# A 24th buffer for expert weights in place of the attention's probabilities, and a mixer ring of four chunks instead of five

## The reference, cut to what matters

```python
proj = h @ w_in                       # 1024 x 7184, then conv, recurrence, attention
merged = sigmoid(gate_lru) * (y_lru @ w_lru_out) + sigmoid(gate_fox) * (y_fox @ w_fox_out)
x = x + merged @ w_o
...
for e in range(N_EXPERTS):            # 32
    gu = t @ w_gate_up[e] + b_gate_up[e]               # 1024 x 2048 weights
    gate = jnp.minimum(gu[:, :D_FF], SWIGLU_LIMIT)
    up = jnp.clip(gu[:, D_FF:], -SWIGLU_LIMIT, SWIGLU_LIMIT)
    y = ((up + 1.0) * gate * sigmoid(SWIGLU_ALPHA * gate)) @ w_down[e] + b_down[e]   # 1024 x 1024
    out = out + combine[:, e:e + 1] * y
```

## Time and profile before

| what | us |
|---|---|
| median of three runs (lowest, highest) | 1183.79 (1182.74, 1183.94) |
| the profiled execution | 1183.51 |
| its span, first to last instruction | 1181.73 |
| TensorE busy in the span | 1150.8 (97%) |
| VectorE, ScalarE, GpSimd busy | 339.2, 271.0, 28.3 |
| transferred by DMA | 452.92 MB, mean 383 GB/s |

### The profile page before, as it was taken

One profiled execution on the slowest core, in us unless ns is written; L12 is line 12 of the kernel. 1 busy time (PEld: TensorE's weight loads), 2 busy tenths in 40 slices (PEclk: granted clock), 3 DMA queues, 4 the chain that ended last, 5 costly groups with the idle time before them and its releaser, 6 DMA issues.

```text
span 1181.7 us, 14466 instructions
## 1 busy us (share of the span) xinstructions
PE 1150.8 (97%) x6297; PEld 590.1 (50%) x6297; DVE 339.2 (29%) x663; ACT 271.0 (23%) x459; POOL 28.3 (2%) x37
## 2 busy tenths in 40 slices
PE   9999999999999999999999999999999999999987
PEld 9998999995333333333433333333333333333322
DVE  6578987663111010102111010101010101010102
ACT  7767766353100100000101010010000000000002
POOL 1001212000000000000000000000000000000000
PEclk9999999999999999999999999999999999999999
DMA  9769766789999999999999999999999999999995
GB/s 294 205 222 310 241 219 214 250 312 385 427 427 428 428 427 434 431 430 429 429 430 432 426 430 430 430 428 431 431 429 428 431 431 428 430 425 428 429 422 242
DMA packets 73285, 452.92 MB, mean 383 GB/s; under 512 B 7194, under 2 KB 46466, under 8 KB 52100
## 3 DMA queue, kind: packets, MB, share of 16 engines
q1 hardware_dynamic: 72944, 451.67, 93.8%
q10 hardware_dynamic: 276, 0.30, 0.1%
HBM read 450.88 MB, written 1.07 MB: 382 GB/s over the span
## 4 chain that ended last, share of the span: by engine, by line
PE 72%; DMA 26%; DVE 1%; ACT 0%; issue 0%; POOL 0%; POOLq 0%; DVEq 0%; ACTq 0%
PE pj L1604 24%; DMA quad<-in_w_gate_up 20%; PE pj L1367 16%; PE gb L1634 13%; DMA pair<-in_w_gate_up 3%; DMA slot<-in_w_down 3%; PE gb L1574 2%; PE s L1641 2%; PE pt L1641 2%; PE ga L1574 2%; PE pj L1618 1%; PE pj L1340 1%; PE pj L1580 1%; PE gb L1623 1%; PE ga L1634 1%; PE pj L1295 1%
## 5 line engine op out<-in xcount | busy, mean ns | idle before, releaser
L1604 PE MATMUL pj<-quad,GL 128*64 128x512 f32 x1280 | 285.1, 601 | 15.0 <-DMA quad<-in_w_gate_up 14.8
L1187 DVE TENSOR_SCALAR x_sb<-pj 128x512 f32<-128x512 f32 x32 | 22.1, 692 | 699.7 <-PE pj L1604 699.7
L1604 PEld LDWEIGHTS pj<-quad,GL 128*64 128x64 f32 x1280 | 89.9, 138 | 199.9 <-issue 173.3
L1634 PE MATMUL gb<-quad,x_sb 128*64 128x512 f32 x640 | 141.7, 595 | 0.0
L737 ACT ACTIVATE x_sb<-x_sb 128x512 f32<-128x512 f32 x32 | 20.2, 630 | 487.6 <-DVE x_sb L1187 487.6
L1604 PE MATMUL pj<-pair,GL 128*64 128x512 f32 x576 | 126.6, 595 | 3.5 <-DMA pair<-in_w_gate_up 3.5
L1367 PE MATMUL pj<-hT_hi,w_hi 128*128 128x256 f32 x424 | 120.7, 285 | 0.0
L1367 PE MATMUL pj<-hT_hi,w_lo 128*128 128x256 f32 x424 | 119.8, 283 | 0.0
L1367 PE MATMUL pj<-hT_lo,w_hi 128*128 128x256 f32 x424 | 117.9, 278 | 0.0
L875 DVE TENSOR_TENSOR w_lo<-mix,w_hi 128x1024 fp32r<-128x1024 f32 x79 | 95.4, 1249 | 34.1 <-ACT w_hi L559 33.2
L1634 PEld LDWEIGHTS gb<-quad,x_sb 128*64 128x64 f32 x640 | 44.2, 137 | 84.9 <-issue 84.9
(11 more groups left out here) (369 smaller groups left out, 1118.7 us busy)
## 6 DMA issues: line engine op xcount, KB each, us to landing
quad<-in_w_gate_up SPq DMA_DIRECT2D x40, 4096.0 KB, 38.7
quad<-in_w_down SPq DMA_DIRECT2D x20, 4096.0 KB, 39.3
pair<-in_w_gate_up SPq DMA_DIRECT2D x36, 2048.0 KB, 20.1
pair<-in_w_down SPq DMA_DIRECT2D x14, 2048.0 KB, 17.2
mix<-in_w_in SPq DMA_DIRECT2D x27, 1024.0 KB, 5.8
slot<-in_w_gate_up SPq DMA_DIRECT2D x21, 1024.0 KB, 8.2
slot<-in_w_down SPq DMA_DIRECT2D x14, 1024.0 KB, 22.9
slot<-in_w_down SPq DMA_DIRECT2D x12, 512.0 KB, 8.6
```

The costliest lines, as they stand in the source:

```text
L1187: v.tensor_scalar(gate, pj[0][:, :], LIMIT, None, ALU.min).then_inc(gate_ready, 1)
L1604: last = mm(pj[q // 2][h:h + SLOTS, :], hg[:, c, i, :], w[:, q * 512:(q + 1) * 512], start=(pair == 0 and c == 0), stop=(c == GU_CHUNKS - ...
L1634: last = mm(to[h:h + SLOTS, :], actT[:, f % 4, f // 4, :], w[:, a * D + q * 512:a * D + (q + 1) * 512], start=False, stop=(f == KT - 1))
```

## The change

- The ring has four mixer buffers. Chunk c's load waits for chunk c - 4 instead of c - 5. The fifth buffer becomes `spare8`, which is free from the start.
- The attention's probabilities (`L`, `PT`), which had a room of their own, are put in a buffer `att` of the slab, which becomes an expert place once the attention is over. There are 24 places, and 13 instead of 11 loads in `EARLY`.
- `b_gate_up` is no longer split. It is loaded in four transfers of 64 KB after load 13, and multiplied as float32 with 64 rows instead of 128. The one-hot matrix comes from a table `half_pick` that GpSimd makes at the start.
- `b_down` is no longer added per expert. It is loaded late, in the middle of the expert stage, into a place that is idle by then, and four matmuls (`add_down_bias`, in experts 17 and 18) add combine weights times `b_down` to the result.
- What gave room for this is moved: the sigmoid of the activation goes to a PSUM bank, `selW` to the room that it left, `tri` and `ones`, `h2T_tail` and `rows` to other rooms.

```diff
-MIX_RING = 5
+MIX_RING = 4
...
-N_PLACES = 23
-PAIR_AT = [1, 3, 5, 7, 9, 19, 21, 11, 13, 15, 17]
+N_PLACES = 24
+PAIR_AT = [0, 2, 4, 6, 8, 10, 20, 22, 12, 14, 16, 18]
 SINGLES = 12
-QUAD_AT = [7, 19, 11, 15, 1]
-FIRST = [0] + [p + i for p in PAIR_AT for i in range(2)]
+QUAD_AT = [0, 4, 8, 20, 12]
+FIRST = [p + i for p in PAIR_AT for i in range(2)]
+COMB_AT = 16
...
-EARLY = {12: 0, 14: 1, 16: 2, 18: 3, 20: 4, 22: 5, 24: 6, 29: 7, 33: 8, 36: 9, 37: 10}
+EARLY = {12: 0, 14: 1, 16: 2, 18: 3, 20: 4, 22: 5, 24: 6, 26: 7, 29: 8, 33: 9, 36: 10, 37: 11, 38: 12}
+IDLE_PLACES = range(16, 20)
...
-        in_order = ["spare", "spare2", "spare3", "spare4", "spare5", "spare6", "spare7", "lg", "k", "v", "q", "xc", "mix2",
-                    "mix3", "whi0", "r", "i", "whi1", "mix4", "mix0", "hl", "mix1", "lp"]
+        in_order = ["spare", "spare2", "spare3", "spare4", "spare5", "spare6", "spare7", "spare8", "lg", "k", "v", "q", "xc",
+                    "mix1", "mix2", "whi0", "r", "i", "whi1", "mix3", "att", "mix0", "hl", "lp"]
...
-        probs_at = room("probs", 2 * 4 * 2 * 3 * P)
+        probs_at = at["att"]
...
+            free_after[probs_at] = lambda: sp.wait_ge(o_psum, HEADS)
...
             load_expert(len(EARLY))
-            for i in range(4):
-                sp.dma_start(bgu_raw[i * N_EXP:(i + 1) * N_EXP, :].rearrange("e (q n) -> e q n", q=2),
...
+            sp.wait_ge(logits_ready, HEADS)
+            for q in range(4):
+                sp.dma_start(bgu[q * N_EXP:(q + 1) * N_EXP, :], b_gate_up[:, q * 512:(q + 1) * 512]).then_inc(late_loaded, 16)
...
+                if load == BDN_LOAD:
+                    sp.wait_ge(chunk_done, MIX_CHUNKS + LAST_USE + 1)
+                    sp.dma_start(bdn, b_down[:, :]).then_inc(late_loaded, 16)
                 load_expert(load)
...
+            for b in range(4):
+                block_rows = slice(b * N_EXP, (b + 1) * N_EXP)
+                ins = g.tensor_copy(half_pick[block_rows, :, b % 2], pick[block_rows, 0:N_EXP])
...
-            g.tensor_tensor(bgu[:, :], bgu_raw, bgu_part[:, :].bitcast(F32), ALU.subtract).then_inc(bias_split, 1)
...
-                act.activation(sig, gate, ACT.Sigmoid, scale=ALPHA).then_inc(sig_ready, 1)
+                act.activation(to[:, :], gate, ACT.Sigmoid, scale=ALPHA).then_inc(sig_ready, 1)
...
-                    mm(pj[b][:, :], onehot[:, i, :], bgu[:, b * 512:(b + 1) * 512], start=start, stop=False, skip_group_check=not start)
+                    half = slice(b * 2 * N_EXP, (b + 1) * 2 * N_EXP)
+                    mm(pj[b][:, :], onehot[half, 2 * i:2 * i + 2, :].rearrange("p h s -> p (h s)"), bgu[half, :], start=start,
+                       stop=False, skip_group_check=not start)
...
-            def down_bias(i, to=gb):
-                mm(to[:, :], onehot[:, i, :], bdn[:, :], start=True, stop=False)
+            def add_down_bias(t):
+                for h in range(2):
+                    mm(acc[t][h][:, :], combT[:, t * P:(t + 1) * P], bdn[:, h * 512:(h + 1) * 512], start=False, stop=True,
...
```

More of the change, by code:

```diff
@@ L50 @@
 SCRATCH = 1024
-N_PLACES = 23
-PAIR_AT = [1, 3, 5, 7, 9, 19, 21, 11, 13, 15, 17]
+N_PLACES = 24
+PAIR_AT = [0, 2, 4, 6, 8, 10, 20, 22, 12, 14, 16, 18]
 SINGLES = 12
-QUAD_AT = [7, 19, 11, 15, 1]
-FIRST = [0] + [p + i for p in PAIR_AT for i in range(2)]
+QUAD_AT = [0, 4, 8, 20, 12]
+FIRST = [p + i for p in PAIR_AT for i in range(2)]
+COMB_AT = 16
 QUAD_FROM, QUAD_TO = EXP_CHUNKS * 8, EXP_CHUNKS * (N_EXP - 4)
 def plan():
-    loads = [(h, 1, FIRST[h % N_PLACES]) for h in range(N_PLACES + 1 + SINGLES)]
-    for turn, h in enumerate(range(N_PLACES + 1 + SINGLES, QUAD_FROM, 2)):
+    loads = [(h, 1, FIRST[h % N_PLACES]) for h in range(N_PLACES + SINGLES)]
+    for turn, h in enumerate(range(N_PLACES + SINGLES, QUAD_FROM, 2)):
         loads.append((h, 2, PAIR_AT[(turn + SINGLES // 2) % len(PAIR_AT)]))
@@ L85 @@
         LOAD_OF[_h + _m], PLACE_OF[_h + _m] = _i, _p + _m
-EARLY = {12: 0, 14: 1, 16: 2, 18: 3, 20: 4, 22: 5, 24: 6, 29: 7, 33: 8, 36: 9, 37: 10}
+EARLY = {12: 0, 14: 1, 16: 2, 18: 3, 20: 4, 22: 5, 24: 6, 26: 7, 29: 8, 33: 9, 36: 10, 37: 11, 38: 12}
+IDLE_PLACES = range(16, 20)
+LAST_USE = max(h for h, p in PLACE_OF.items() if p in IDLE_PLACES)
+BDN_LOAD = next(i for i, (h, _, _) in enumerate(LOADS) if h >= 12 * EXP_CHUNKS)
 NVEC = 72
@@ L160, in hybrid_block @@
         pick = sb("pick", [P, N_EXP + 2])
-        rest_row = sb("rest_row", [P, 1])
-        same_half = sb("same_half", [P, P])
-        rows = sb("rows", [NVEC, P])
+        half_pick = sb("half_pick", [P, N_EXP, 2])
+        rows = alias("rows", [NVEC, P], F32, bias_at + 4 * 3 * P)
         vec = sb("vec", [P, NVEC + KT])
@@ L343, in _ @@
             free_after = {mix_at[i]: (lambda c=MIX_CHUNKS - MIX_RING + i: sp.wait_ge(chunk_done, c + 1)) for i in range(MIX_RING)}
-            for name in ("spare", "spare2", "spare3", "spare4", "spare5", "spare6", "spare7"):
+            for name in ("spare", "spare2", "spare3", "spare4", "spare5", "spare6", "spare7", "spare8"):
                 free_after[at[name]] = lambda: None
@@ L409, in _ @@
             load_expert(len(EARLY))
-            for i in range(4):
-                sp.dma_start(bgu_raw[i * N_EXP:(i + 1) * N_EXP, :].rearrange("e (q n) -> e q n", q=2),
-                             b_gate_up.rearrange("e (q h n) -> h e q n", q=2, h=2)[i // 2]).then_inc(late_loaded, 16)
-            for i in range(4):
-                sp.dma_start(bdn_raw[i * N_EXP:(i + 1) * N_EXP, :], b_down[:, i // 2 * 512:(i // 2 + 1) * 512]).then_inc(late_loaded, 16)
+            sp.wait_ge(logits_ready, HEADS)
+            for q in range(4):
+                sp.dma_start(bgu[q * N_EXP:(q + 1) * N_EXP, :], b_gate_up[:, q * 512:(q + 1) * 512]).then_inc(late_loaded, 16)
             for load in range(len(EARLY) + 1, BY_HALVES[0]):
@@ L785, in _ @@
                     Y_copy(n)
+                if n == COMB_AT:
+                    act.wait_ge(combT_psum, 1)
+                    act.activation(combT, pj[0][0:N_EXP, 0:S], ACT.Identity).then_inc(combT_ready, 1)
             sigmoid_of(N_EXP - 1)
@@ L840, in _ @@
             v.memset(wf[:, :, HEADS:], 0.0).then_inc(preset, 1)
-            for i in range(4):
-                v.memset(rest_row[i * N_EXP:(i + 1) * N_EXP, :], float(i % 2)).then_inc(rest_row_ready, 1)
-            dve.wait_ge(rest_row_ready, 4)
             dve.wait_ge(vec_psum, 1)
@@ L1620, in transpose_act, with transpose_comb @@
                 last.then_inc(act_transposed, 1)
-            def down_bias(i, to=gb):
-                mm(to[:, :], onehot[:, i, :], bdn[:, :], start=True, stop=False)
+            def transpose_comb():
+                for t in range(TT):
+                    last = nc.tensor.transpose(pj[0][0:N_EXP, t * P:(t + 1) * P], comb[:, t, :], ident[:, :])
+                last.then_inc(combT_psum, 1)
+            def add_down_bias(t):
+                for h in range(2):
+                    mm(acc[t][h][:, :], combT[:, t * P:(t + 1) * P], bdn[:, h * 512:(h + 1) * 512], start=False, stop=True,
+                       skip_group_check=True)
             def down(i, chunk_at, actT=actT, to=gb, which=range(DN_CHUNKS), second_half=None):
```

118 lines of the change are left out of this document (54 added, 64 removed).

## The result

| | before | after |
|---|---|---|
| median of the runs, us | 1183.38 (1182.48 to 1184.43, 15 runs) | 1186.29 (1183.69 to 1188.77, 15 runs) |
| profiled execution / its span, us | 1183.51 / 1181.7 | 1186.57 / 1184.8 |

The ratio is 1.0025, 95% interval 1.0018 to 1.0032: the change makes the kernel 0.25% slower, 2.9 us. The forecast was 1181.7, with a range that ended at 1183.9. The sign is wrong, and the time lies outside the range.

The account below looks back on a forecast made before the run. The mixer stage was taken as TensorE-bound, the expert stage as bound by the full DMA stream at 2.46 us per MiB. Terms -2.46 + 0 + 0.4 = -2.06 took 1183.51 to 1181.45, plus 0.28: 1181.7 us, range 1180.4 to 1183.9.

Parts of the forecast that it names:

- One more place: Expert weight stream: one MiB more lands early, in the mixer stage's slack, taking 2.46 us from the end.
- the mixer's end: Loads 14 to 19 and half loads: the full stream starts neither earlier nor later, 0 us, between -0.6 and +0.6.
- the four `b_gate_up` transfers: SP's queue at the mixer's end: four small bias transfers take 1.2 us, so load 19 lands at 270.5.
- The 3.8 us: Alternative estimate for the four `b_gate_up` transfers, from the skill's 0.95 us each; load 19 would land at 273.1.
- `b_down`: Its 128 KB leave the slack and enter the full expert stream: +0.4 us, between 0.31 and 0.75.
- The ring of four: Mixer stage: chunk loads get two chunks of TensorE's time, at least 11.58 us, against 10.2 for the slowest: price 0.
- the ring runs dry: Rival, mixer stage: chunk loads take over two chunks, TensorE stands still at early loads, 1189 to 1196 us; chance 0.07.
- TensorE per expert: Expert stage: new bias pair takes 0.57 us, -0.67 to +0.31 per expert, covered by the stream, so 0 us.
- TensorE's first wait for a weight transfer: Expert stage: comes at some 630 us instead of 718, with no effect on the end.
- The end: After the last landing: 19.3 us of matmuls and norm stay unchanged; TensorE has 1.2 us to spare at that landing.
- Load 19: Last early load at the mixer's end: lands at 270.5, bounds 269.9 to 271.6, where load 18 landed at 270.7.

Follow-up runs that it names:

- Run 9: Changed kernel with the gate-weight loads behind chunk 6 and `b_down`'s load left out, zeros in its place: 1180.92 us, ratio 0.9979 to the kernel before.
- run 1: Changed kernel with the four gate-weight loads issued behind chunk 6's load instead of chunk 7's: 1182.13 us, ratio 0.9992 to the kernel before.
- run 6: Changed kernel with gate-weight loads behind chunk 6 and `b_gate_up` loads behind chunk 38's load instead of load 13: 1183.86 us, ratio 1.0008 to the kernel before.
- run 4: Kernel before with the ring of four alone and the gate-weight loads behind chunk 6's load: 1184.23 us, ratio 1.0009 to the kernel before.
- Run 2: Kernel before, ring of five, with the gate-weight loads behind chunk 8's load instead of chunk 7's: 1186.75 us, ratio 1.0033.
- 15: Changed kernel, gate-weight loads behind chunk 6, down bias left out, its bytes loaded as 128 rows of 1 KB, order "q e", into an idle place: 1181.55 us.
- 12: Changed kernel, gate-weight loads behind chunk 6, `b_down` loaded as 128 rows of 1 KB in order "q e" and used: 1181.66 us, ratio 0.9991.
- 11: Changed kernel, gate-weight loads behind chunk 6, down bias left out, its bytes loaded as 128 rows of 1 KB, memory order, into an idle place: 1180.83 us.
- 13: Changed kernel, gate-weight loads behind chunk 6, `b_down` loaded as 128 rows of 1 KB in memory order and used: 1181.54 us, ratio 0.9986.
- 14: Changed kernel, gate-weight loads behind chunk 6, down bias left out, its bytes loaded as 64 rows of 2 KB into an idle place: 1182.29 us.
- run 10: Changed kernel, gate-weight loads behind chunk 6, `b_down` issued on ScalarE's queue during expert 14 instead of by SP: 1182.41 us, ratio 0.9994.

## Why the prediction was wrong

*One more place, -2.46.* Right, as far as the runs can tell. Run 9, which has the place but no `b_down`, is 2.4 us below the kernel before (1180.92 against 1183.32), with half loads 0.5 earlier (266.88). In run 1 the 24th MiB lands 3.3 us earlier than before (222.7 against 226.0), of which 0.7 come from a mixer that was as much ahead in that trace (half loads at 266.75, not 267.42). That leaves 2.7 for the place and the mixer's end together, where the prediction had 2.46 and 0, with bounds of 0.6. Its 1.2 us for the four `b_gate_up` transfers is near, too: with them moved away load 18 lands 1.1 us earlier (266.4 in run 6, 267.5 in run 1). The 3.8 us that the prediction set beside it are not seen. They came from the 0.95 us of the Trainium skill ("DMA: Bandwidth & Descriptors", section "Bandwidth"), which is measured with 128 partitions and transfers issued by GpSimd, while these are issued by SP, to 32 partitions each; and the page says "descriptor-dominated" of transfers under 64 KB.

*`b_down`, +0.4, bounds 0.3 to 0.75.* Mis-sized: 1.2 by the times and 1.3 by the traces of runs 1 and 9. The rate of the stream and that of eight transfers in the slack were both the wrong row: the same 128 KB cost 1.3 us as 32 rows and 0.1 as 128, so bytes alone don't set the price. The words "rows are 4 KB long like those of the half loads" looked at the length of a row and not at the 32 partitions they go to.

*The ring of four, price 0.* This step failed, and it set the sign. "Chunk c's load has two chunks of TensorE's time instead of three to land" is true, and no run shows a wait for a chunk. But the step priced only the loads that go into the ring. Every issue behind such a load on SP's queue moves with it, and four of them, the gate weights behind chunk 7, had 3.4 us of cover (landed at 37.42, wanted at 40.84) against a move of one chunk, 5.3 us (42.74 - 37.42). The 1.9 us that are missing and the 0.5 by which TensorE came earlier are the wait of 2.4 in the trace, and behind it the clock was at 0.50, another 1.45. The prediction did ask what is queued behind a later wait, at the mixer's end and for `b_down`, but not along the whole ring. The rival "the ring runs dry" named the right part and the wrong mechanism, and its 1189 to 1196 was too high.

*TensorE per expert, worth 0.* Right in effect, with the size wrong: 0.05 us saved per expert where 0.67 were forecast, with a bound of 0.11. A bias pair takes 1.13 and not 0.57, and two experts 53.96 us, against 54.06 in the earlier trace rows:

```profile
361.65 1.13 PE L1577 MATMUL pj<-bgu,onehot 64*128 64x512 f32 x4
```

```profile
361.65:415.61 53.96, 53.96 (x262) 20.46 (x260) 8.14 (x18) 5.25 (x11) 0.00 (x0) 1.00 1.01 428
```

The pair, two products, is four rows of the profile; so the scatter's four rows were two products as well, and the prediction, which took them for four, halved the price. Hence TensorE's first wait for a weight transfer came at 721 us and not at 630. Since the stream covers it, the end doesn't show it.

*The end.* Right. At the last landing of the chain TensorE had 0.36 us to spare and now has 1.31, 0.95 more, where 1.2 in all were forecast. From there to the end of the span it is 18.8 us, not 19.3; the half microsecond lies behind the last of VectorE's work, where the output is stored, and that part varies (4.6 us before, 4.1 after, 5.4 in run 1). The row of the last wait, after:

```profile
1166.12 1.94 PE L1639 MATMUL ga<-slot,x_sb 128*64 128x512 f32 x8 [1.31 <-DMA slot<-in_w_down]
```

**The sum, corrected:** -2.46 for the place, +1.25 for `b_down` (between the 1.2 and the 1.3) and +3.5 for the mixer's delay make +2.3; the medians differ by 2.9, with an interval of 2.1 to 3.8. Load 19 is no further term: in the kernel after it lands at 276.07, 6.1 us later than in run 1, but by the 24th MiB the two are 4.5 apart, and their half loads were issued 4.2 apart. For run 1 the same sum, with a mixer 0.7 ahead instead of the delay, is -1.9; measured was -1.15 (interval -1.9 to +0.1). What is left over is 0.6 and 0.7 us, and the ring alone left 1.0 in run 4. Run 2, the one edit that keeps five buffers, leaves nothing (+3.5, with half loads 3.7 later). So the ring may cost up to a microsecond beyond the gate loads. Each of these remainders is within the noise, and no run shows where it would come from: this part stays open.

## What to carry to other kernels

When a ring or a wait in a queue changes, list every instruction that the queue issues behind it, not only those that the ring feeds, and compare the spare of each with the whole step by which it moves. A small load that rides behind a ring's load is best hung on the earliest wait that it can stand. And in a queue that is full to the end, a small transfer's bytes are not its price; in these runs it was cheapest spread over all 128 partitions in memory order.

## What the runs showed of the hardware

- 128 KB in a full stream cost 1.3 us as 32 rows of 4 KB, 1.8 as 64 rows of 2 KB, 0.1 as 128 rows of 1 KB in memory order and 0.6 to 1.0 with the rows in the other order (growths above, less the 4.9 of run 9; traces with the same form differ by up to 0.7). The Trainium skill ("SBUF — State Buffer", section "Door 1: The DMA port swizzle (why `[64,N]` ≈ `[32,N]`)") has a transfer's bandwidth depend on how many of 16 ports its partitions reach, and partitions 0 to 63 reach half of them, as 0 to 31 do; the traces agree, since 64 cost no less than 32. For the other order the Trainium skill ("DMA: Bandwidth & Descriptors", section "Why a DMA increments its semaphore by 16 and not by 1") has the slowest dimension of the access pattern, here the 4 of "q e", limit the number of DMA engines. The traces of runs 15 and 12 agree: the semaphore of this transfer has five updates there, one 1.1 us after the issue and four between 22 and 25 us after it, and sixteen in runs 1, 11, 13 and 14. That fewer engines are why this order costs 0.6 to 1.0 is argued, not shown.
- Issued by ScalarE, the same transfer saved nothing in the times (1182.41 against 1182.13), while the trace shows no step of its size (run 10): open.
- After an idle 2.37 us in the mixer the granted clock was 0.50 (1.2 GHz) from 45 to 47 us and 1.00 again from 48 us; the 32 matmuls after 2.41 us in the earlier trace rows had shown the same in the expert stage.
- Executions of one kernel spread by 2.0 us (before) to 5.1 us (after). Among the traces with the edit of run 1, all with half loads issued between 266.7 and 267.5, the 56th MiB stands anywhere from 223.5 to 227.1 on the scale of the table. What decides it is open.
